# The opening of a diffusion layer: order of loads, condition rows, one section of the modulation and one norm on other engines

## The reference

```
mod_x = silu(c) @ ada_w + ada_b            # 1 x 6144: shift, scale, gate, twice
mod_c = silu(c_ctx) @ ada_w + ada_b        # the same for the context
sh1, sc1, g1, sh2, sc2, g2 = split(mod_x, 6);  ch1, cc1, ... = split(mod_c, 6)
hc = rms(ctx, norm1) * (1 + cc1) + ch1     # 256 x 1024
hx = rms(x, norm1) * (1 + sc1) + sh1       # 1024 x 1024
zx = hx @ w_in                             # columns for a long convolution, attention, gates
```

## Time and profile before

| | |
|---|---|
| median of 3 runs | 2223.07 us (2223.02 to 2225.51) |
| profiled execution | 2225.76 us |
| its span, first to last instruction | 2223.6 us |
| mean granted TensorE clock | 0.981 |
| TensorE / VectorE / ScalarE / GpSimd busy | 96% / 75% / 52% / 9% |

### The profile page before, as it was taken

One profiled execution on the slowest core, in us unless ns is written; L12 is line 12 of the kernel. 1 busy time (PEld: TensorE's weight loads), 2 busy tenths in 40 slices (PEclk: granted clock), 3 DMA queues, 4 the chain that ended last, 5 costly groups with the idle time before them and its releaser, 6 DMA issues.

```text
span 2223.6 us, 27445 instructions
## 1 busy us (share of the span) xinstructions
PE 2129.8 (96%) x10117; PEld 1709.5 (77%) x10117; DVE 1668.5 (75%) x1720; ACT 1160.0 (52%) x1229; POOL 198.0 (9%) x69
## 2 busy tenths in 40 slices
PE   7999999989999999999399999999999999999998
PEld 2998888866577776688278888888888888888886
DVE  3667765167553898753788988998989889898986
ACT  3521222156400221321167777777777778777784
POOL 0000000000000000300011101111011111011100
PEclk9999999999999999999699999999999999999999
DMA  8134454030111133643589999999999999999993
GB/s 307 58 97 161 137 194 143 38 129 15 21 75 35 42 114 115 208 174 103 196 305 358 381 398 391 380 379 380 390 397 383 378 378 380 401 390 377 380 381 116
DMA packets 183292, 538.34 MB, mean 242 GB/s; under 512 B 15231, under 2 KB 57355, under 8 KB 182708
## 3 DMA queue, kind: packets, MB, share of 16 engines
q1 hardware_dynamic: 172768, 505.67, 60.8%
q0 software_dynamic: 4752, 16.78, 2.9%
q10 hardware_dynamic: 5700, 14.90, 1.7%
HBM read 501.66 MB, written 35.65 MB: 242 GB/s over the span
## 4 chain that ended last, share of the span: by engine, by line
PE 49%; DVE 2%; DMA 0%; issue 0%; ACT 0%; POOL 0%; POOLq 0%
PE p_y L247 5%; PE p_y L249 5%; PE p_a L247 5%; PE p_a L249 5%; PE p_a L248 5%; PE p_y L248 5%; PE p_b L248 5%; PE p_b L249 5%; PE p_b L247 5%; PE p_t L2462 1%; PE p_t L2453 1%; DVE idx_rows L2417 1%; DVE late L2420 0%; DVE vals L2415 0%; DMA g1row<-xn_dram,idx_e 0%
## 5 line engine op out<-in xcount | busy, mean ns | idle before, releaser
L2358 DVE TENSOR_TENSOR r_lo<-ring,r_hi 128x2048 fp32r<-128x2048 f32 x384 | 865.8, 2287 | 62.9 <-ACT r_hi L2317 56.0
L2317 ACT ACTIVATE r_hi<-ring 128x2048 fp32r<-128x2048 f32 x384 | 731.0, 1915 | 154.6 <-PE p_b L249 75.5
L247 PE MATMUL p_y<-r_hi,a_hi 128*128 128x512 f32 x512 | 205.3, 401 | 0.0
L247 PE MATMUL p_a<-r_hi,x_hi 128*128 128x512 f32 x512 | 202.5, 396 | 1.0 <-DVE x_lo L2369 1.0
L249 PE MATMUL p_y<-r_hi,a_lo 128*128 128x512 f32 x512 | 200.0, 391 | 0.0
L249 PE MATMUL p_a<-r_hi,x_lo 128*128 128x512 f32 x512 | 199.8, 390 | 0.0
L248 PE MATMUL p_a<-r_lo,x_hi 128*128 128x512 f32 x512 | 199.2, 389 | 0.0
L248 PE MATMUL p_y<-r_lo,a_hi 128*128 128x512 f32 x512 | 199.2, 389 | 0.0
L247 PE MATMUL p_b<-r_hi,x_hi 128*128 128x512 f32 x512 | 199.2, 389 | 0.0
L248 PE MATMUL p_b<-r_lo,x_hi 128*128 128x512 f32 x512 | 199.2, 389 | 0.0
L249 PE MATMUL p_b<-r_hi,x_lo 128*128 128x512 f32 x512 | 199.2, 389 | 0.0
(11 more groups left out here) (352 smaller groups left out, 3648.5 us busy)
## 6 DMA issues: line engine op xcount, KB each, us to landing
ring<-in_w_gate SPq DMA_DIRECT2D x128, 1024.0 KB, 8.5
ring<-in_w_up SPq DMA_DIRECT2D x128, 1024.0 KB, 8.2
ring<-in_w_down SPq DMA_DIRECT2D x128, 1024.0 KB, 11.8
w_raw<-in_w_in SPq DMA_DIRECT2D x17, 1024.0 KB, 6.2
ada_rest<-in_ada_w SPq DMA_DIRECT2D x16, 1024.0 KB, 5.3
ada<-in_ada_w SPq DMA_DIRECT2D x8, 1024.0 KB, 15.2
gate_dram<-zs ACTq DMA_DIRECT2D x16, 512.0 KB, 2.6
x_normed<-gate_dram SPq DMA_DIRECT2D x16, 512.0 KB, 4.3
```

The lines of the kernel that those rows point to most:

```text
L247: pe.matmul(out, a_hi, b_hi, start=start, stop=False)
L2317: act.activation(r_hi[:, i % PARTS], ring[:, i % RAW], ACT.Copy).then_inc(hi_ready, 1)
L2358: dve.tensor_tensor(r_lo[:, i % PARTS], ring[:, i % RAW], r_hi[:, i % PARTS].bitcast(F32), ALU.subtract).then_inc(lo_ready, 1)
```

## The change

1. `c` and `c_ctx` are loaded first and alone by SyncE, turned and copied ahead of the other rows; those are loaded by ScalarE's queue and turned after section 0. TensorE runs 6 and 8 filling matmuls of the identity around it.
2. The filter network's 15 small loads go from ScalarE's queue to GpSimd's.
3. Large loads: section 0, x 0 and 1, section 3, x 2 and 3, section 1, section 2, weights 0, x 4 and 5, x 6 and 7, context, weights 1, 2.
4. Section 3 is summed off TensorE: VectorE for `c` (eight steps on 128x512), for `c_ctx` ScalarE's products with GpSimd's additions, then eight matmuls with a column of ones.
5. Unit 0's weights are split in four pieces; the low parts are GpSimd's.
6. The token norm is in three parts (tiles 0 to 3, 4 to 7, context); the scaling of tiles 4 to 7 is GpSimd's.

The diff, cut to its core (the filter layers' two places between the sections before are left out, as are the semaphores; `SUMMED` is 3, `NEAR_T` 4, `KD` 8, `NT` 8, `NTC` 2):

```diff
 (sync)
-                at = 0
-                for name, n in (("ada_b", 48), ("norm1", 8), ("norm2", 8), ("c", 8)):
-                    sp.dma_start(rows1[at:at + n, :], A[name]...).then_inc(rows_in, 16)
-                sp.dma_start(rows1[at:at + 8, :], A["c_ctx"]...).then_inc(rows_in, 16)
...
+                sp.dma_start(rows1[64:72, :], A["c"]...).then_inc(c_in, 16)
+                sp.dma_start(rows1[72:80, :], A["c_ctx"]...).then_inc(c_in, 16)
                 load_section(0, 0)
                 load_section(0, 1)
                 load_x(0)
-                load_section(1, 0)
-                load_section(1, 1)
+                load_section(SUMMED, 0)
+                load_section(SUMMED, 1)
                 load_x(1)
-                load_section(2, 0)
-                load_x(2)
-                load_section(2, 1)
-                load_x(3)
-                load_section(3, 0)
-                load_section(3, 1)
+                for i in (1, 2):
+                    load_section(i, 0)
+                    load_section(i, 1)
...
                 load(0)
+                load_x(2)
+                load_x(3)
                 load_x(4)
                 load(1)
                 load(2)
 (gpsimd)
+                pool.dma_start(feat, A["feat"]).then_inc(f_in, 16)
+                pool.wait_ge(f_zero, 2)
+                for h in range(2):
+                    pool.dma_start(w1[:, h, FH * h:FH * h + FH], A["filt_w1"][0]).then_inc(f_in, 16)
+                for i, n in enumerate(("filt_b1", "filt_b2", "filt_b3", "filt_freq")):
+                    for h in range(2):
+                        pool.dma_start(vec[FH * h:FH * h + FH, i:i + 1], A[n].rearrange("o h -> h o")).then_inc(f_in, 16)
+                for h in range(2):
+                    for t, n in ((w2, "filt_w2"), (w3, "filt_w3")):
+                        pool.dma_start(t[FH * h:FH * h + FH, FH * h:FH * h + FH], A[n][0]).then_inc(f_in, 16)
+                for k in range(1, KD):
+                    pool.wait_ge(product, k + 1)
+                    if k > 1:
+                        pool.wait_ge(sum_step[1], k - 1)
+                    pool.tensor_tensor(acc1[:, 1], acc1[:, 1], hf[:, k % 3], ALU.add)
+                for q in range(KD // 2):
+                    pool.wait_ge(w_hi_first, q + 1)
+                    k = slice(2 * q, 2 * q + 2)
+                    pool.tensor_tensor(w_lo[0][:, k], w[:, 0, k], w_hi[0][:, k].bitcast(F32), ALU.subtract)
+                pool.wait_ge(norm_step, 12)
+                for t in range(NEAR_T, NT):
+                    pool.tensor_scalar(x[:, t, :], x[:, t, :], r0[:, t:t + 1], None, ALU.mult).then_inc(xn_far, 1)
 (scalar)
-                for t in range(NT):
+                for t in range(NEAR_T // 2):
                     square(t)
-                    if t == 5:
-                        sine(0)
-                act.wait_ge(norm_step, 1)
-                act.activation(rt[:, 0:NT], ss[:, 0:NT], ACT.Sqrt).then_inc(root_ready, 1)
+                act.wait_ge(sil_ready, 1)
+                for k in range(KD):
+                    if k % (KD // 2) == 0:
+                        act.wait_ge(ada_in[2 * SUMMED + k // (KD // 2)], 16)
+                    if k >= 4:
+                        act.wait_ge(sum_step[1], k - 3)
+                    act.activation(hf[:, k % 3] if k else acc1[:, 1], ada[:, SUMMED, k, :], ACT.Copy, scale=sil[:, 1, k:k + 1])
+                    if k in (3, 5):
+                        square(NEAR_T // 2 + (k == 5))
+                roots(0, NEAR_T, 1)
+                sine(0)
                 high_part(0)
+                for t in range(NEAR_T, NEAR_T + 3):
+                    square(t)
                 act.wait_ge(mod_ready, 4)
...              for i, (h, k) in enumerate(GROUPS):
-                    if i in (4, 6):
-                        square(NT + (i == 6))
+                    if i == 1:
+                        square(NT - 1)
+                    if i == 3:
+                        roots(NEAR_T, NT, 7)
+                    if i in (6, 8):
+                        square(NT + (i == 8))
 (vector)
+                def section_sums():
+                    a = acc1[:, 0]
+                    for k in range(KD):
...
+                        if k == 0:
+                            ins = dve.tensor_scalar(a, ada[:, SUMMED, 0, :], sil[:, 0, 0:1], None, ALU.mult)
+                        else:
+                            dve.wait_ge(sum_step[0], k)
+                            ins = dve.scalar_tensor_tensor(out=a, in0=ada[:, SUMMED, k, :], scalar=sil[:, 0, k:k + 1], in1=a,
+                                                           op0=ALU.mult, op1=ALU.add)
...
+                section_sums()
+                mean_squares(0, NEAR_T)
                 copy_section(0)
-                copy_section(1)
                 dve.wait_ge(f_in, 16 * 15)
                 filter_layer(0)
+                copy_section(1)
+                token_roots(0, NEAR_T, 1, 1)
+                norm_tokens(0, NEAR_T)
                 copy_section(2)
-                norm_tokens(0, 5)
-                copy_section(3)
...              for i in range(len(GROUPS)):
-                    if i == 1:
-                        weights_low(0)
                     if i == 3:
-                        norm_tokens(5, NT)
+                        mean_squares(NEAR_T, NT)
+                    if i == 4:
+                        token_roots(NEAR_T, NT, 7, 2)
 (tensor)
                 pe.wait_ge(consts, 3)
-                pe.wait_ge(rows_in, 80)
-                pe.wait_ge(rows2_in, 48)
+                fill(6)
+                pe.wait_ge(c_in, 32)
+                pe.transpose(p_rows[:, 64:80], rows1[64:80], ident[64:80, 64:80]).then_inc(c_turned, 1)
+                fill(8)
                 pe.wait_ge(sil_ready, 1)
-                for s_ in range(SECTIONS):
+                for s_ in range(SUMMED):
                     for k in range(KD):
+                        if s_ == 1 and k == KD // 2:
+                            pe.wait_ge(f_in, 16 * 15)
+                            pe.wait_ge(cols_ready, 2)
+                            pe.matmul(p_f[:], w1[:, 0, :], feat[:, 0:512], start=True, stop=False)
+                            pe.matmul(p_f[:], w1[:, 1, :], feat[:, 512:L], start=False, stop=True).then_inc(fz_ready, 1)
+                        if s_ == 2 and k == KD // 2:
+                            pe.wait_ge(sin_ready, 1)
+                            pe.matmul(p_f[:], w2, hid[:], start=True, stop=True).then_inc(fz_ready, 1)
...
+                    if s_ == 0:
+                        turn_rows()
+                    if s_ == 1:
+                        turn_section(0)
+                for v in range(2):
+                    pe.wait_ge(sum_ready[v], 1)
+                    for c in range(4):
+                        at = 2 * (4 * SUMMED + c) + v
+                        pe.matmul(p_mod[:, at:at + 1], acc1[:, v, P * c:P * c + P], ones[:, 0:1], start=True, stop=True)
+                turn_section(1)
+                turn_section(2).then_inc(mod_t, 1)
...              for i, (h, k) in enumerate(GROUPS):
-                    pe.wait_ge(xn_ready, tiles[-1] + 1)
+                    if h == 1:
+                        pe.wait_ge(xn_far, NT - NEAR_T)
+                    else:
+                        pe.wait_ge(xn_ready, NEAR_T if h == 0 else NEAR_T + NTC)
```

More of the change, by code:

```diff
@@ L263, in front @@
     SECTIONS = 2 * D // 512
+    SUMMED = SECTIONS - 1
+    NEAR_T = NT // 2
     EARLY = 8
@@ L343, in front @@
         w_hi_ready, w_lo_ready = sem("w_hi_ready"), sem("w_lo_ready")
+        w_hi_first, w_lo_first = sem("w_hi_first"), sem("w_lo_first")
+        product = sem("section_product")
+        sum_step, sum_ready = ([sem(f"{n}{v}") for v in range(2)] for n in ("sum_step", "sum_ready"))
         group_done, evacuated = sem("group_done"), sem("evacuated")
@@ L555, in square, with roots @@
                     act.activation(junk, x[:, t, :], ACT.Square, accum_out=ss[:, t:t + 1]).then_inc(ss_ready, 1)
-                for t in range(NT):
+                def roots(a, b, steps):
+                    act.wait_ge(norm_step, steps)
+                    act.activation(rt[:, a:b], ss[:, a:b], ACT.Sqrt).then_inc(root_ready, 1)
+                for t in range(NEAR_T // 2):
                     square(t)
-                    if t == 5:
-                        sine(0)
-                act.wait_ge(norm_step, 1)
-                act.activation(rt[:, 0:NT], ss[:, 0:NT], ACT.Sqrt).then_inc(root_ready, 1)
+                act.wait_ge(sil_ready, 1)
[4 more added lines that the diff above has]
+                        act.wait_ge(sum_step[1], k - 3)
+                    act.activation(hf[:, k % 3] if k else acc1[:, 1], ada[:, SUMMED, k, :], ACT.Copy, scale=sil[:, 1, k:k + 1])\
+                       .then_inc(product, 1)
+                    if k in (3, 5):
+                        square(NEAR_T // 2 + (k == 5))
+                roots(0, NEAR_T, 1)
+                sine(0)
```

(20 more changed lines are left out.)

98 lines of the change are left out of this document (47 added, 51 removed).

## The result

The changed kernel took 2234.02 us, median of 4 runs (2233.23 to 2235.1); the kernel before, on the same chip, 2223.05 (2222.76 to 2225.51). The ratio is 1.0044, 95% interval 1.0032 to 1.0056: slower by 11.0 us, where 2.4 were forecast, and above the range's end of 2232. The profiled execution took 2233.79 us, its span is 2232.0.

The account below looks back on a forecast made before the run. TensorE was taken as the bound, so only its arrival at the row at 66.11 counts. 1.5 + 0.9 = 2.4 us later gives 2228.2 profiled, 2225.5 for the median; 8 in 10 range 2219 to 2232.

Parts of the forecast that it names:

- D: Norm of tiles 4 to 7 on GpSimd: 1.3 us a tile, 5.2 in all, group 8 at 61.2, 1.5 us later.
- Rival 3: GpSimd's tiles cost 2.37 us each, TensorE idles over 6 us and drops to half clock: 2231; chance 0.10.
- A: Load order: first section's load starts 2.3 us earlier, the 7th transfer lands at 24.5.
- B: TensorE up to the modulation: section 1 starts cold, costing 2.0 us; first modulation at 47.4, 1.1 us later.
- C: Sine and first weights' low parts ready on time; first projection 2.2 us after the first modulation, at 49.6.
- E: From group 8 to the row at 66.11: 6.45 us now, plus 0.9 for the second context square.
- Rival 1: Before group 8: GpSimd isn't the limit, tiles at 0.68 us, clock up; 2220.9, or 2219 to 2220; chance 0.20.
- Rival 2: GpSimd's queue of 15 filter loads delays TensorE's filter matmuls; 2239 at 2.67 us each; chance 0.10.

Follow-up runs that it names:

- experiment 8: Kernel of experiment 2 with section 1 loaded before the later tiles and the engines' lists following that order; 2231.9 us, ratio 1.0037.
- experiment 6: Kernel before with first weights split in four, low parts by GpSimd: 2222.77 us; with condition rows first and small loads moved too: 2222.78 us; both ratio 0.9992.
- experiment 4: Changed kernel with GpSimd scaling tiles 4 to 7 in product form: 2230.09 us, ratio 1.0028; before it, one run with four forms, one per tile.
- experiment 2: Changed kernel with VectorE scaling tiles 4 to 7 and 44 idle matmuls ahead of section 1; 2228.16 us, ratio 1.0017.

## Why the prediction was wrong

**The failing step is D, the price of a GpSimd tile.** The prediction took 1.3 us, "a little over half of the latter, since one input is read instead of two", with bounds of 0.68 and 2.37. Measured: 2.84 in the median, 11.82 us for the four against 5.2. That is 6.6 of the 9.5 us by which the row came later than forecast (77.98 - 66.11 = 11.9 against 2.4). The bound from above was wrong too: the addition with two inputs was held to be the dearer form, and the run of four forms shows the reverse. The Trainium skill (GPSIMD Engine Reference, Engine selection) calls GpSimd's one-input operations "roughly line-rate". Of the copy that holds here (1.04 us for 1024 elements a partition, alone); of the multiplication by a scalar it doesn't, at 2.77 and 2.84.

The rest of D was right: the root's table load that returns (55.32 in ScalarE's timeline, 1.28 us), the start of GpSimd 8.4 us after the first modulation (8.5 forecast), TensorE idle in front of group 8, and GpSimd's tiles as releaser. The growth of GpSimd's tiles beside VectorE's low parts, some 0.8 us that the sum left out, came to 0.5, on the first tile. Rival 3 had the mechanism, with a price still too low.

**A, the load order: 2.3 us mis-sized, 1.0 measured.** SyncE's first big load is indeed issued at 1.55 us in place of 3.81. But what arrives isn't 2.3 earlier: ScalarE's squares of tiles 0 and 2 after, the second of these against the row of 24.06 in the earlier trace rows:

```profile
15.22 1.06 ACT L581 ACTIVATE ub<-x_in 128x1024 f32<-128x1024 f32 x1 [9.92 <-DMA x_in<-in_x]
...
23.11 1.06 ACT L581 ACTIVATE ub<-x_in 128x1024 f32<-128x1024 f32 x1 [2.65 <-DMA x_in<-in_x]
```

Tile 2's transfer plus the 2.71 us step gives 25.8, and section 1 starts at 25.84, not 24.5. With the filter loads back on ScalarE's queue, tile 0 comes 1.2 earlier and section 1 0.2. What holds up the rest wasn't settled.

**B, the first modulation: 49.55 against 47.4.** Of the 2.15 us, 1.3 are the transfer above, and 0.4 the cold half of section 1 (6.03 us, 2.4 over the warm 3.60, where 2.0 were reckoned). The remainder lies behind the last turn: its transposes came at a granted clock of 0.57 (window from 48.30 to 51.70; 16 in 3.37 us, where the kernel before has 16 in 2.29 at a clock of 1.00), so that VectorE waited 0.59 for the first of them. The mechanism, TensorE starting section 1 cold because nothing stands before it, was right, and the run with 44 idle matmuls gave 2.19 us back for it. Eight column sums at 1.9 us were right to 0.05, and so was the conclusion that taking section 3 off TensorE doesn't bring the modulation forward.

**C held, but for its times.** The weights' low parts were no limit (wait of 0.17 at the first projection), and it came 2.3 us after the modulation (2.2 forecast). What C and D had seen of the collision between GpSimd and VectorE, was priced for GpSimd's side and left out of the sum for VectorE's. VectorE's seven products with addition for section 3, after:

```profile
18.37 10.07 DVE L712 SCALAR_TENSOR_TENSOR qkv<-ada,sil,qkv 128x512 f32<-128x512 f32 x7
```

That is 1.44 us each, 1.64 in the median and 0.75 for the shortest. In the changed kernel it is hidden in the long wait for section 1. Beside GpSimd's low parts the norm of tiles 0 to 3 stretches as well, to 5.75 us where four of the earlier trace rows would take 2.7; it ends at 45.8, just when TensorE has finished section 2, so it cost nothing here. In the order of experiment 8 both lie in the chain that decides. The Trainium skill (SBUF — State Buffer, SBUF: two separate sides) says that a VectorE instruction with two SBUF inputs needs a port pair that GpSimd uses as well, and that this is an exclusive lock, held for a whole instruction. By it VectorE waits out GpSimd's instruction, and no more than that. Beside GpSimd's products and subtractions of two tensors the runs agree: an instruction on 128x8 that takes 0.17 us alone took 0.90 and 1.30 in experiment 6, where one low part takes GpSimd 1.27, and a low part of VectorE's took up to 2.38 in experiment 4, where a tile takes GpSimd 2.34. Beside the column form they don't: in the changed kernel a tile holds GpSimd for 2.84 us and more, and VectorE's low parts, with their two inputs, took 0.88 us at most. There it was GpSimd's tile that grew, to 3.35. So the runs bear the page out for GpSimd's forms with two tensors, and not for its column form.

**E: 1.6 in place of 0.9.** From group 8 to the row it takes 77.98 - 69.90 = 8.08 us, where 6.45 + 0.9 was reckoned. The run with VectorE's tiles has 7.67 there, the one with idle matmuls 8.15, with 2.58 us of waiting for ScalarE. In the latter the granted clock is 0.99 from group 8 to the row and ScalarE is busy for 8.05 us of that stretch, so there its chain sets the length; its extra square was a right term, and too small. In the changed kernel the clock is 0.50 up to 75.1 us and the row itself waits for nobody, so there the clock may make up the same time; how the 1.6 us divide wasn't separated.

The terms add up: D 6.6, B with A in it 2.15, E 0.7, together 9.45, and C nothing. The rule that a microsecond before the row moves all behind it held for the changed kernel (11.9 at the row, 11.9 at the first store, 11.0 in the median). It is not exact: in experiments 2 and 8 TensorE is at half clock behind the row, and the first store moves by 1.5 and 2.7 us more than the row. The shift of the first store and that of the median agree within 2 us, about what the comparison can resolve, but for experiment 4 (+8.6 and +5.1), for which the record has no reason.

**The rivals.** Rival 1 fell with the tiles' price. Rival 2 fell: GpSimd's 15 loads were issued between 2.11 and 10.1 us, 0.54 us each, and TensorE's filter matmuls waited for none of them. Its chance of 0.10 bought width where none was needed, while D's bound from above, taken from an operation of another form, cut the range short where it was.

## What to carry to other kernels

Take an engine's price for an instruction from a row of that very form; where there is none, a row of another form is no upper bound, whatever the count of its inputs. Work moved off a busy engine to an idle one has to be followed to its consumer: here four tiles that VectorE scales in 2.74 us went to an engine that needs 11.82, and TensorE was waiting for them. And moving work to GpSimd isn't free for VectorE: look at what VectorE does in the same microseconds, above all at small instructions in the chain, which can wait for a whole one of GpSimd's when that one reads two tensors. And take the effect of an edit at a place behind the next wait: in experiment 2 the row won 2.2 us and the first store 0.75.

## What the runs showed of the hardware

- GpSimd, 128x1024, 32-bit: multiplication by a column or a constant 2.84 and 2.77 us, product of two tensors 1.90 (one of them a spread column), copy 1.04. VectorE does the column form in 0.68.
- Beside GpSimd's subtractions of two tensors (1.27 us each), a VectorE instruction of 0.17 us took up to 1.30; beside its column form, five scalings of a tile took VectorE 5.89 us in place of 3.40.
- VectorE's low part of a group (128x512, two inputs, 0.69 us) took up to 2.38 beside GpSimd's product form and 0.88 at most beside its column form.
- Small plain loads are issued from GpSimd's queue at 0.54 us each (15 in 8 us), against 0.38 on SyncE.
- With the first load issued 2.26 us earlier, the sixth transfer of 1 MB came only 0.95 us forward (square at 23.11 in place of 24.06).
